# Mixer A of a hybrid network on one core: the low part of the queries made later, one query group ahead of the first scores, output groups started on x's parts

## The chip, the core and the metric

The kernel runs on one core of a Trainium2 chip. Five engines work side by side, each through its own queue in order: PE (TensorE), DVE (VectorE), ACT (ScalarE), POOL (GpSimd) and SP (SyncE, which issues the transfers). They wait for each other by semaphores. The metric is device time in microseconds, the median of several runs.

## What is computed

The reference is a network of two blocks. The part that the change touches is mixer A, the first layer's grouped attention with axial rotation, on 512 tokens of x and 256 of a context (model width 1024, 16 heads of 64):

```python
px = hx @ w_in
q, k, v, z = ...                                   # columns of px
q = apply_axial_rope(rms_norm(q, q_g), cos, sin)
k = apply_axial_rope(rms_norm(k, k_g), cos, sin)
k_all = concatenate([kc, k]); v_all = concatenate([vc, v])
s = einsum(q, k_all) * ATTN_SCALE
o = softmax(s) @ v_all                             # blocks of 128 queries
yx = (o * silu(z)) @ w_out
...                                                # the context: own queries, over kc and vc alone
x = x + g_x * yx ; ctx = ctx + g_c * yc
```

All is in 32-bit floats. Products that need full precision are split into a high and a low part (fp32r): a projection is three matmuls, high x high, low x high and high x low.

## The kernel before

A plan is made first: a list of items such as ("score", "a", n), written in order by ordinary Python, and each engine's program then takes from it the items in which it has a share. So one order sets five queues. The change touches mixer A's attention.

*Steps.* There are 8 pairs of heads (0 to 7) and for each pair 6 tiles of 128 queries, four of x (against 768 keys, "large") and two of the context (256 keys, "small"). Step n is tile n % 6 of pair n // 6, so 48 steps, 0 to 47. `attention` runs the softmax as a pipeline: in step n PE makes score n (L1530, 12 matmuls, 6 in a small tile), the outputs of step n - 2 ("pv", L1565) and the transposes of the probabilities of n - 1 ("turn", L1540), for two heads h. DVE takes the maximum (L2154) and its negative (L2163), ACT the exponential with its sum (L1814), DVE the reciprocal (L2170), POOL scales (L2544); turned probabilities are copied from PSUM by ACT (L1824) and DVE (L2179); DVE keeps the output, times the gate (L2190). Scores of both heads fill PSUM banks 0 to 3, a single buffer, so a score waits for the exponentials of the step before. Turns use banks 4 and 5, and outputs also bank 5. A step needs its own PE work and leaves PE idle unless something fills the gaps.

*Fill.* The generator `fill_a` yields projection blocks ("proj": 3 matmuls, one of 8 k; L1442 to L1444; 512 columns for x, j = 0, and 256 for the context, j = 1). `fill_in` draws from it in the two halves of a step (before and after the turn of head 1), up to a share of the remaining work by the step's weight (1.0, small tiles 0.7); `PAUSE` ends a half's filling at once, and `BLOCK` says that nothing may be drawn. For pair p = 1 to 7 `fill_a` makes the query group (pair, 0), (pair, 1), then the gate group (pair, 0), (pair, 1). In the gate group hang the query's further steps: sums (L1507, L2114, POOL's power L2532), rotation (L1513, L2118, POOL's L2537, and the sum on DVE L2124), the high part (ACT, L1796), the low part (DVE, L2128), and the gate: tanh (ACT, L1804), product (DVE, L2134). After the low part the pair counts as ready and its first score may be made. "mod" units (L1455 and L1463) ride along. Pair 0's groups are made before the steps.

*Output groups.* At the end `begin_out` begins the output projection ("aout", m = 0 and 1, x's columns): for each k, the gated outputs of pair k are split into parts ("parts": ACT casts the high part, L1776; POOL for even k, L2518, and DVE for odd k, L2074, subtract the low one) into the buffers that held the projections' input. Hence parts wait until the gate groups are done with it.

*Weights.* A unit of weights is loaded by SP, then split in quarters: ACT casts (L1726), POOL subtracts (L2477). `tick` puts a quarter into the plan; the load of the unit after next follows the fourth quarter.

## Time and profile before

| | |
|---|---|
| median of 3 runs | 1638.76 us (1638.26 to 1641.87) |
| profiled execution | 1637.41 us, span from first to last instruction 1635.7 us |
| PE busy | 1551.2 us, 95% |
| DVE, ACT, POOL busy | 740.2, 623.5, 658.7 us |
| attention of mixer A | 107.9 to 459.2 us of the span |

The profile is of one execution. Rows of the timeline give an instruction's start, its duration, its form, how many of that form follow each other, and in brackets how long the engine was idle before it and on what it waited. Rows of windows give the busy time of each engine in a stretch and PEclk, the granted TensorE clock as a share of full speed.

### The profile page before, as it was taken

The numbers are of one execution on the slowest core, as the hardware profiler recorded it, in microseconds if no ns is written. First come the engines' busy times: TensorE is split into PE (matmuls) and PEld (weight loads), VectorE is DVE, ScalarE is ACT, GpSimd is POOL, SyncE is SP. The second block draws the span as 40 slices with busy tenths as digits, with TensorE's granted clock in tenths as the row PEclk, the third lists the DMA queues.
The fourth block names the chain that finished last, engine by engine and source line by source line (L and its number), as shares of the span: only waits on it lengthen the run. The fifth ranks groups of instructions, "written<-read, shape, count | busy, mean of one in ns | idle before, by whom it ended". The sixth has DMA issues, their size and how long they took to land.

```text
span 1635.7 us, 25366 instructions
## 1 busy us (share of the span) xinstructions
PE 1551.2 (95%) x10018; PEld 1227.2 (75%) x10018; DVE 740.2 (45%) x1717; ACT 623.5 (38%) x1303; POOL 658.7 (40%) x640
## 2 busy tenths in 40 slices
PE   5999999999898999999998899999999999999997
...
GB/s 396 47 60 52 31 49 53 53 52 27 72 123 103 78 78 78 104 78 110 72 104 52 78 92 73 100 52 103 52 78 78 90 66 78 52 52 27 78 98 57
DMA packets 22438, 129.80 MB, mean 79 GB/s; under 512 B 2480, under 2 KB 2608, under 8 KB 8368
## 3 DMA queue, kind: packets, MB, share of 16 engines
q1 hardware_dynamic: 22176, 127.92, 21.9%
...
## 4 chain that ended last, share of the span: by engine, by line
PE 81%; DVE 8%; ACT 3%; POOL 3%; issue 3%; DMA 1%; SPq 0%; POOLq 0%; DVEq 0%; ACTq 0%
PE PS L1442 15%; PE PS L1444 14%; PE PS L1443 14%; PE PS L1565 6%; PE PS L1540 6%; PE PS L1523 4%; PE PS L1696 3%; PE PS L1437 3%; PE PS L1438 3%; PE PS L1439 3%; PE PS L1530 3%; DVE sm L2154 2%; PE PS L1706 2%; PE PS L1618 1%; PE PS L1610 1%
## 5 line engine op out<-in xcount | busy, mean ns | idle before, releaser
L2477 POOL TENSOR_TENSOR WL<-W,WH 128x512 fp32r<-128x512 f32 x280 | 367.4, 1328 | 321.7 <-ACT WH L1726 321.4
L1442 PE MATMUL PS<-HX,WH 128*128 128x512 f32 x1008 | 420.5, 417 | 11.3 <-DVE LX L2067 3.7
L1444 PE MATMUL PS<-HX,WL 128*128 128x512 f32 x1008 | 398.6, 395 | 0.0
L1443 PE MATMUL PS<-LX,WH 128*128 128x512 f32 x1008 | 398.3, 395 | 0.0
L1442 PEld LDWEIGHTS PS<-HX,WH 128*128 128x128 f32 x1008 | 192.5, 191 | 62.7 <-issue 17.9
L1444 PEld LDWEIGHTS PS<-HX,WL 128*128 128x128 f32 x1008 | 192.1, 191 | 42.7
L1443 PEld LDWEIGHTS PS<-LX,WH 128*128 128x128 f32 x1008 | 192.7, 191 | 36.7 <-issue 3.4
L1726 ACT CAST WH<-W 128x512 fp32r<-128x512 f32 x296 | 172.0, 618 | 51.6 <-PE PS L1439 23.7
L1814 ACT ACTIVATE AR<-PS,sm 128x768 f32<-128x768 f32 (+4 forms) x160 | 115.7, 723 | 173.8 <-DVE sm L2159 101.1
L2154 DVE TENSOR_REDUCE sm<-PS 128x1 f32<-128x512 f32 (+4 forms) x224 | 149.9, 669 | 44.8 <-PE PS L1530 40.3
L2544 POOL TENSOR_SCALAR AR<-AR,sm 128x768 f32<-128x768 f32 (+1 forms) x96 | 77.1, 804 | 186.8 <-DVE sm L2170 186.8
L1540 PE MATMUL PS<-C,AR 128*128 128x128 f32 x608 | 101.4, 284 | 10.0 <-DVE AR L2190 9.9
L2544 POOL TENSOR_SCALAR XC<-XC,sm 128x512 f32<-128x512 f32 x64 | 45.0, 703 | 163.0 <-DVE sm L2170 163.0
L1824 ACT COPY AR<-PS 128x512 f32<-128x512 f32 (+1 forms) x112 | 62.2, 555 | 108.9 <-PE PS L1540 107.9
L1565 PE MATMUL PS<-AR 128*64 128x128 f32 x1408 | 96.8, 283 | 5.3 <-DVE AR L2179 3.6
L1540 PEld LDWEIGHTS PS<-C,AR 128*128 128x128 f32 x608 | 68.9, 141 | 43.4 <-issue 22.6
L1814 ACT ACTIVATE XC<-PS,sm 128x512 f32<-128x512 f32 x64 | 44.2, 690 | 145.0 <-DVE sm L2159 145.0
L1437 PE MATMUL PS<-WH,HX 128*128 128x256 f32 x320 | 94.9, 297 | 0.8 <-POOL WL L2477 0.8
L1565 PEld LDWEIGHTS PS<-AR 128*64 128x64 f32 x1408 | 77.2, 139 | 23.4 <-issue 11.8
L1439 PE MATMUL PS<-WL,HX 128*128 128x256 f32 x320 | 91.2, 285 | 0.0
L1438 PE MATMUL PS<-WH,LX 128*128 128x256 f32 x320 | 91.2, 285 | 0.0
L2547 POOL TENSOR_SCALAR AR<-AR,sm 128x128 f32<-128x128 f32 (+3 forms) x64 | 39.2, 612 | 111.8 <-DVE sm L2170 109.3
...
## 6 DMA issues: line engine op xcount, KB each, us to landing
...
```

Of the source, the lines that this page charges most:

```text
L1437: e.matmul(o, xh, wh, start=(k == 0), stop=False)
L1438: e.matmul(o, xl, wh, start=False, stop=False)
L1439: t = e.matmul(o, xh, wl, start=False, stop=(k == 7))
L1442: e.matmul(o, wh, xh, start=(k == 0), stop=False)
L1443: e.matmul(o, wh, xl, start=False, stop=False)
L1444: t = e.matmul(o, wl, xh, start=False, stop=(k == 7))
L1540: t = e.transpose(o[:, j * 128:j * 128 + 128], s.pb[h][:, (q0 + j) * 128:(q0 + j) * 128 + 128], c("id"))
L1565: t = e.matmul(s.out[h], s.values[h][j], s.pt[h][:, j * 128:j * 128 + 128], start=(j == 0 and s.first), stop=(j == nv - 1 and s.final))
L1726: e.copy(WH[:, PART[n], a:z], W[:, n % 2, a:z]).then_inc(*s_wh.by(n, q))
L1814: e.activation(s.pb[h][:, 0:s.n], PS[:, s.score[h]:s.score[h] + s.n], ACT.Exp, bias=smn[:, i % 4:i % 4 + 1], scale=(1.0 if s.scale is None ...
L2154: e.tensor_reduce(mx, x, AX.X, ALU.max).then_inc(*s_max.by(name, n, h))
L2477: e.tensor_tensor(WL[:, d, a:z], W[:, n % 2, a:z], WH[:, d, a:z].bitcast(F32), ALU.subtract).then_inc(*s_wl_pool.by(n, q))
```

## The change

Three things in mixer A. In `fill_a` the low part of a pair's queries is written behind block k = 5 of the gate group of the context instead of k = 1, and most pauses are gone. The query group (1, 0) is drawn ahead of the first score: an `AHEAD` mark is yielded behind it, and the caller draws up to the mark. The output groups are begun by a new `begin_out_a`: the part of x of pair 0 and 1 is made while the last gate group of the context still runs (parts of x now wait for the gate group of x alone), the parts of x are always two k ahead of their blocks, a context part follows its block, and there are no pauses. The work handed to `attention` is 890.9 instead of 946.8 units of 100 columns, over steps whose weights sum to 43.2: 20.6 instead of 21.9 for a step of weight 1. (One unit is three matmuls of 100 columns.)

```diff
-        def parts_a(k):
-            for j, (lo, hi) in enumerate(FULL):
-                after = [(s_gated, ("a", j)) if k == 7 else (s_post, ("a", 6 * k + 5)), (s_proj, ("az", 7, 1))]
-                parts("o", k, j, zT.at(k, lo, hi), after, "pool" if k % 2 == 0 else "dve")
+        def parts_a(k, j):
+            lo, hi = FULL[j]
+            after = [(s_gated, ("a", j)) if k == 7 else (s_post, ("a", 6 * k + 5)), (s_proj, ("az", 7, j))]
+            parts("o", k, j, zT.at(k, lo, hi), after, "pool" if k % 2 == 0 else "dve")
+
+        def begin_out_a():
+
+            un = Unit("aout", 0)
+            led = {(m, 0): bank(FA.take(("aout", m, 0), (s_res, ("aout", m, 0)))) for m in (0, 1)}
+            for k in range(2, 9):
+                if k < 7:
+                    yield from until(lambda: k in done_a)
+                    parts_a(k, 0)
+                for m in (0, 1):
+                    yield from pj(("aout", m, 0), un, 0, T, 128 * m, "o", led[m, 0], (k - 2,))
+                parts_a(k - 2, 1)
+            begun["aout"] = un, led
...
             for pair in range(1, 8):
                 yield from query_group(pair, 0, FX, {2: ride_mm, 6: ride_tr})
-                yield PAUSE
+                if pair == 1:
+                    yield AHEAD
                 yield from query_group(pair, 1, FC)
...
-                yield from gate_group(pair, 1, FC, {1: lambda: query_low(pair), **({3: ride_mm_x, 6: ride_tr} if pair == 7 else {})})
-                yield PAUSE
-            yield from begin_out("aout", "o", parts_a, done_a, FA)
+                last_ = {2: lambda: parts_a(0, 0), 3: ride_mm_x, 4: lambda: parts_a(1, 0), 6: ride_tr} if pair == 7 else {}
+                yield from gate_group(pair, 1, FC, {**last_, 5: lambda: query_low(pair)})
+            yield from begin_out_a()
...
-        attention("a", [s for pair in range(8) for s in steps_a(pair)], SA, TA, PbA, PTbA, OA, fill_a(), (8 * 14 * (T + LC) + 14 * T) / 100 + 5 * 3, posted_a, scored_a.add)
+        fill_ = fill_a()
+        while next(fill_) != AHEAD:
+            pass
+        attention("a", [s for pair in range(8) for s in steps_a(pair)], SA, TA, PbA, PTbA, OA, fill_, (8 * 14 * (T + LC) + 6 * T) / 100, posted_a, scored_a.add)
...
-        parts_a(7)
+        parts_a(7, 0)
+        parts_a(7, 1)
```

The changed kernel has 18 more lines, so its lines from here on are numbered 18 higher. ACT, around the first exponential (its table load; L1814 before, L1832 in the change), before:

```order
L1796 CAST XX_parts<-AR 128x768
L1726 CAST WH<-W 128x512 x2
L1804 ACTIVATE AR<-PS 128x256
L1814 ACT_TABLE_LOAD
L1814 ACTIVATE AR,sm<-PS,sm 128x768 x2
L1733 COPY AR<-PS 128x256
L1824 COPY AR<-PS 128x512
```

and in the change, from the high part of pair 0 (L1796, now L1814):

```order
L1814 CAST XX_parts<-AR 128x768
L1744 CAST WH<-W 128x512 x2
L1822 ACTIVATE AR<-PS 128x256
L1751 COPY AR<-PS 128x256
L1744 CAST WH<-W 128x512 x2
L1809 ACTIVATE AR<-PS 128x512
L1832 ACT_TABLE_LOAD
L1832 ACTIVATE AR,sm<-PS,sm 128x768 x2
L1744 CAST WH<-W 128x512 x2
L1809 ACTIVATE AR<-PS 128x256
```

A mod unit's row, two casts of weights (L1744) and the square of the raw queries (L1809) now stand ahead of it, and two more casts behind it.

DVE, from the gate of x (L2134) of pair 6 to the first maximum behind its low part (L2128, writing XX_parts), before:

```order
L2134 SCALAR_TENSOR_TENSOR AR<-AR,PS 128x512
L2154 TENSOR_REDUCE sm<-PS 128x1
L2163 TENSOR_SCALAR sm<-sm 128x1
L2190 SCALAR_TENSOR_TENSOR AR<-PS,AR 128x128
L2179 COPY AR<-PS 128x256
L2154 TENSOR_REDUCE sm<-PS 128x1
L2163 TENSOR_SCALAR sm<-sm 128x1
L2170 RECIPROCAL sm<-sm 128x1
L2128 TENSOR_TENSOR XX_parts<-AR,XX_parts 128x768
L2170 RECIPROCAL sm<-sm 128x1
L2154 TENSOR_REDUCE sm<-PS 128x1
```

and in the change (gate L2152, low part L2146), from the output kept in the last step of pair 5 on:

```order
L2208 SCALAR_TENSOR_TENSOR AR<-PS,AR 128x128
L2197 COPY AR<-PS 128x256
L2172 TENSOR_REDUCE sm<-PS 128x1
L2181 TENSOR_SCALAR sm<-sm 128x1
L2188 RECIPROCAL sm<-sm 128x1
L2142 TENSOR_TENSOR AR<-AR 128x512
L2188 RECIPROCAL sm<-sm 128x1
L2152 SCALAR_TENSOR_TENSOR AR<-AR,PS 128x512
L2146 TENSOR_TENSOR XX_parts<-AR,XX_parts 128x768
L2172 TENSOR_REDUCE sm<-PS 128x1
L2181 TENSOR_SCALAR sm<-sm 128x1
```

Before, a step's maxima and two reciprocals (L2170) stood between gate and low part on one side and the score's first maximum on the other; now the low part stands behind both reciprocals (L2188) and the gate, directly ahead of the maximum (L2172) of the score that needs it.

PE, from score 43 on, before (score L1530, outputs L1565, turns L1540, block L1442 to L1444):

```order
L1530 MATMUL PS<-AR_parts,XX_parts 128x512 x6
L1530 MATMUL PS<-AR_parts,XX_parts 128x256 x6
L1565 MATMUL PS<-AR 64x128 x4
L1540 MATMUL PS<-C,AR 128x128 x12
L1530 MATMUL PS<-AR_parts,XX_parts 128x512 x6
L1530 MATMUL PS<-AR_parts,XX_parts 128x256 x6
L1565 MATMUL PS<-AR 64x128 x12
L1540 MATMUL PS<-C,AR 128x128 x6
L1442 MATMUL PS<-HX,WH 128x512
L1443 MATMUL PS<-LX,WH 128x512
L1444 MATMUL PS<-HX,WL 128x512
L1442 MATMUL PS<-HX,WH 128x512
```

and in the change (L1548, L1583, L1558, L1460 to L1462):

```order
L1548 MATMUL PS<-AR_parts,XX_parts 128x512 x6
L1548 MATMUL PS<-AR_parts,XX_parts 128x256 x6
L1583 MATMUL PS<-AR 64x128 x4
L1558 MATMUL PS<-C,AR 128x128 x6
L1460 MATMUL PS<-HX,WH 128x512
L1461 MATMUL PS<-LX,WH 128x512
L1462 MATMUL PS<-HX,WL 128x512
L1460 MATMUL PS<-HX,WH 128x512
L1461 MATMUL PS<-LX,WH 128x512
L1462 MATMUL PS<-HX,WL 128x512
L1558 MATMUL PS<-C,AR 128x128 x6
L1460 MATMUL PS<-HX,WH 128x512
```

Before, score 44 followed the turns of step 43 directly, and the first blocks of the output stood in step 44; now two blocks stand in each half of step 43, and they run out earlier.

## Rows read from the trace of the kernel before

**Rows 1.** The page: busy time, share and instructions of PE and the others.

```profile
PE 1551.2 (95%) x10018; PEld 1227.2 (75%) x10018; DVE 740.2 (45%) x1717; ACT 623.5 (38%) x1303; POOL 658.7 (40%) x640
```

**Rows 2.** Windows: length, busy of PE, PEld, DVE, ACT, POOL; PEclk; DMA share; GB/s.

```profile
107.90:459.20 351.30, 329.28 (x2799) 264.59 (x2797) 183.51 (x487) 170.13 (x364) 151.04 (x150) 0.98 0.15 53
```

**Rows 3.** Waits of PE, 105 to 465 us: in total, times, the longest.

```profile
PE PS L1540 <- DVE AR L2190: 9.9, 12, 2.8
PE PS L1565 <- DVE AR L2179: 3.6, 6, 1.2
```

**Rows 4.** Timeline of PE: rows behind a pause.

```profile
110.03 1.32 PE L1530 MATMUL PS<-AR_parts,XX_parts 64*128 64x512 f32 x12 [1.94 <-DVE AR L2134]
...
145.87 0.44 PE L1540 MATMUL PS<-C,AR 128*128 128x128 f32 x2 [2.81 <-DVE AR L2190]
...
191.35 0.44 PE L1540 MATMUL PS<-C,AR 128*128 128x128 f32 x2 [1.57 <-DVE AR L2190]
...
325.02 1.53 PE L1565 MATMUL PS<-AR 128*64 128x128 f32 x24 [1.08 <-DVE AR L2179]
...
413.61 2.29 PE L1530 MATMUL PS<-AR_parts,XX_parts 64*128 64x512 f32 x12 [2.12 <-DVE XX_parts L2128]
...
427.42 2.29 PE L1530 MATMUL PS<-AR_parts,XX_parts 64*128 64x512 f32 x12 [1.88 <-ACT AR L1814]
...
430.95 2.83 PE L1565 MATMUL PS<-AR 128*64 128x128 f32 x24 [1.25 <-DVE AR L2179]
```

**Rows 5.** Windows: three slow stretches, and a stretch between.

```profile
145.80:151.00 5.20, 5.13 (x32) 4.89 (x32) 2.41 (x8) 1.75 (x5) 1.58 (x2) 0.67 0.42 165
...
413.50:417.00 3.50, 3.39 (x21) 2.67 (x22) 1.06 (x2) 0.00 (x0) 0.00 (x0) 0.51 0.65 272
427.30:435.00 7.70, 6.33 (x44) 5.47 (x45) 3.94 (x8) 3.39 (x8) 5.24 (x5) 0.56 0.00 0
...
190.00:236.00 46.00, 42.50 (x365) 34.28 (x366) 24.46 (x66) 21.65 (x47) 18.37 (x18) 1.00 0.14 47
```

**Rows 6.** Timelines of PE and ACT: scores, second exponentials (ACT) and a block.

```profile
404.11 0.62 PE L1530 MATMUL PS<-AR_parts,XX_parts 64*128 64x256 f32 x6
...
407.64 0.57 ACT L1814 ACTIVATE AR<-PS,sm 128x256 f32<-128x256 f32 x1 [1.51 <-DVE sm L2163]
...
426.19 0.99 ACT L1814 ACTIVATE AR<-PS,sm 128x768 f32<-128x768 f32 x1 [0.75 <-DVE sm L2163]
...
436.51 0.48 PE L1442 MATMUL PS<-HX,WH 128*128 128x512 f32 x1
...
438.08 1.33 PE L1530 MATMUL PS<-AR_parts,XX_parts 64*128 64x512 f32 x12
...
443.34 1.00 ACT L1814 ACTIVATE AR<-PS,sm 128x768 f32<-128x768 f32 x1 [0.25 <-DVE sm L2163]
...
445.10 0.62 PE L1530 MATMUL PS<-AR_parts,XX_parts 64*128 64x256 f32 x6
```

**Rows 7.** Timelines of ACT and DVE: low parts, high part, gate and copy.

```profile
236.95 1.20 DVE L2128 TENSOR_TENSOR XX_parts<-AR,XX_parts 128x768 fp32r<-128x768 f32 x1 [0.18 <-issue]
...
322.59 0.82 ACT L1796 CAST XX_parts<-AR 128x768 fp32r<-128x768 f32 x1
...
323.94 0.69 DVE L2134 SCALAR_TENSOR_TENSOR AR<-AR,PS 128x512 f32<-128x512 f32 x1 [1.87 <-ACT AR L1804]
...
324.55 0.42 DVE L2179 COPY AR<-PS 128x256 f32<-128x256 f32 x1
...
412.51 0.95 DVE L2128 TENSOR_TENSOR XX_parts<-AR,XX_parts 128x768 fp32r<-128x768 f32 x1
```

**Rows 8.** DMA, 95 to 140 us in 40 slices: busy tenths of the 16 engines.

```profile
DMA  0000000000000007697891000000000000000000
```

**Rows 9.** Timeline of PE: the last score and the last outputs.

```profile
452.11 0.62 PE L1530 MATMUL PS<-AR_parts,XX_parts 64*128 64x256 f32 x6
...
458.59 0.66 PE L1565 MATMUL PS<-AR 128*64 128x128 f32 x8 [0.46 <-ACT AR L1824]
```

2 lines of the change are left out of this document (1 added, 1 removed).

## The prediction

> **What bounds the kernel now.** I read the page first, then the busy times by stage, the waits of TensorE and its timeline. [rows 1] PE is busy for 95% of the span. In mixer A's attention, 107.9 to 459.2 us [rows 2], which is all that the change touches, it is busy for 329.3 of 351.3 us, a busy time that overstates its use since pipelined matmuls overlap. So time can only be won from PE's pauses there and from stretches at the lower clock. The waits of PE in this stage come to 21.6 us in seven groups: the first two hold 13.5 [rows 3], the other five, on exponentials, copies, the low part and the gate, 8.1; the timeline shows where the long ones are [rows 4]. Three stretches ran at a lower granted clock [rows 5]: 0.67 over 5.2 us, 0.51 over 3.5 us and 0.56 over 7.7 us, worth 1.7, 1.7 and (its wait of 1.25 us taken out) about 2.8 us of lost work, each behind a pause of 1.9 to 2.8 us. Together 27.8 us are lost in the stage. About 2.5 of that are pauses of 0.2 to 0.3 us that any order has (turns that wait for the kept output after a small tile), so 25.3 us are at stake.
>
> **The limit of a step.** A step has its own PE work, and fill (blocks of projections) between. From score to score the step at 438.08 took 7.02 us with four blocks of 512 columns; two blocks take 1.57 us, from the block at 436.51 to the score at 438.08 [rows 6], 0.69 each and 0.2 for starting, so the own work is some 4.27 us with the starts in it. The next score waits for the second exponential: this ends 6.26 us after the score's start (438.08 to 444.34) [rows 6], and a score follows such an end by 0.24 us (426.19 + 0.99 = 427.18, then the score at 427.42) [rows 4, 6]. So a large tile cannot be under 6.5 us, and needs 2.2 us of fill. The last small tile of a pair (404.11 to 408.21) cannot be under 4.3 us, and has 2.5 us of own work. Fill above these limits costs only itself, and the total of fill is the same in both kernels. What counts is fill that is missing in one step, and waits for the query chain.
>
> **Part 1, a group ahead and the start.** The first score waited 1.94 us for the gate product on VectorE [rows 4]. Now eight blocks and a mod unit stand ahead of it (5.5 and 1.4 us): the wait goes, 1.9 gained. The cost is on ScalarE: two casts of weights and the square stand ahead of the first exponential, and the cast waits for the load that is issued once GpSimd's splits are through, near 111.4. The transfers of this and the next unit run from 111.9 to 119 before [rows 8]; the first has landed at about 116.3, the first exponential comes at about 118.0 instead of 117.4 (107.9 + 6.9 + score 1.3 + maximum 1.2), and PE, with only 2.9 us of fill then, waits about 1.1 us. The third step has two blocks (1.4 us) where 2.2 are needed: 0.8 lost. The chain rotation, high part, gate of pair 1 stands ahead of the fourth step now, where the score is long (1.33 us) and hides nearly all: 0.25. Pair 1 lost 2.81 and 1.7 of clock before. Sum: from 6.45 to 2.15.
>
> **Part 2, pairs 2 to 7.** Pauses are fewer and a step's share of fill is 20.6 instead of 21.9 (by the kernel's own count), so the query chain shifts against the steps. Two mechanisms, both in the trace. First, the gate ahead of something urgent on VectorE: high part 0.82, tanh 0.6, gate 0.69, and then the copy of the turned probabilities, for which PE's outputs waited 1.08 us [rows 4, 7]. Pair 2 gets this form, with the high part only behind the second exponential: 6.26 + 0.75 + 0.6 + 0.7 + 0.4 = 8.7 us, where PE stands ready at 7.1, so 1.6 (its gate wait of 1.57 goes). Pair 3 keeps the old form ahead of a small tile, 0.5 instead of 1.57, since the rotation is done earlier. Second, the low part. In pairs 4 to 7 it now stands on VectorE behind the reciprocal of the step's second exponential, one block ahead of the score that needs it. So this score comes no sooner than 0.15 + 0.94 + 0.15 = 1.24 us behind the end of that exponential, where 0.24 is the old limit, and later where the gate is in front. Worked through the queues: pair 4: the gate delays the maxima, score 24 comes at 11.7 us behind score 22, for 10.0 us of work: 1.7. Pair 5: exponential 4.15, high part to 4.95, tanh 5.5, gate 6.2, low 7.2, score at 7.4; work 5.7: 1.6. Pair 6: high part to 5.5, gate 6.7, low 7.6, score 7.75; work 6.4: 1.35. Pair 7: the low half of a part of x (odd, so on VectorE) waits there for its ScalarE cast at 7.9 and stands ahead of the low part: low 9.5, score 9.6; work 7.9: 1.7. Fill missing at large tiles (1.4 us in steps 33 and 39, 1.8 in step 9, 1.4 in step 13, which is the one behind two small tiles) adds 0.3 and 0.4 (pair 2), 0.7 (pair 3), 0.1 each (pairs 4, 5), 0.8 and 0.8. Sum by pair, before to now: 1.6 to 2.3, 1.65 to 1.2, 1.7 to 1.8, 1.5 to 1.7, 1.2 to 2.15, 2.4 to 2.5: 10.05 to 11.65. These pairs gain nothing; they lose 1.6.
>
> **Part 3, the tail (steps 42 to 47).** Before, steps 42 and 43 have parts but no output blocks, and PE waits 1.88 us for the exponential and 1.25 for a copy that stands behind the parts on VectorE [rows 4], at 1.2 GHz; with the clock (1.7 and 2.8), 0.66 and the last 0.92 it is 9.2. Now the 14 blocks stand in every half. Step 42: the part of k = 3 stands ahead of the next maximum on VectorE and ends near 8.1 us behind score 42, where the maximum could start at 6.9: 1.4 us at the turn. Steps 44 to 46: 0.4, 0.8 (two blocks only), 0.2. Step 47 has no fill left: from its score to the last output it took 7.07 us with 1.37 of blocks and 0.92 of waits [rows 9], so 4.78 of work, while its chain of exponential, reciprocal, scale, turn, copy takes about 6.7: 1.9. Sum 4.7, so 9.2 to 4.7. Moved blocks cost the same where they land.
>
> **The sum.** By places it was 6.45 + 10.05 + 9.2 = 25.7, by the totals 25.3, and I take the smaller; now it is 2.15 + 11.65 + 4.7 = 18.5. For the clock I add 1.5: one drop, as at 145.8 [rows 5], since pairs 7 and step 42 have two pauses of 1.4 to 1.7 us within 10 us. So 20.0 against 25.3: 5.3 us less. The profiled execution took 1637.41 us (span 1635.7), the median is 1.35 above it. Span 1630.4, time 1638.76 - 5.3 = **1633.5 us**. Unknown costs: a low-part wait is between 0 (where the exponential ends early) and 2.1 (the one at 413.61), four of them 0 to 8.4, taken at 6.35; the clock between 0 and 6.2.
>
> **Two rules of the Trainium skill.** [rows 4, 5] Pauses of 0.2 to 1.6 us between 190 and 236 us left the clock at 1.00, that is 2.4 GHz; 1.88 and more had rows at 1.2 GHz behind them, though 1.94 at 110.03 had not. The Trainium skill, "TensorE: Matmul & The Clock Gate", section "A second HAM failure mode: psum-queue depth-cycling", says that frequent micro-idles between groups of matmuls are enough to make the clock oscillate. By that rule the new order, with about as many short waits, would throttle again, which is the slower rival below; by the rows it would not. [rows 7] The low part took 1.20 us at 236.95 and 0.95 at 412.51, with the same operands. The Trainium skill, "GPSIMD Engine Reference", section "Specifications", says that GpSimd shares SBUF interfaces with VectorE and that instructions with two SBUF inputs contend. By it four low parts on the path could cost 0.25 more each, 1.0 in all, and the time would be 1634.5.
>
> **The rivals.** *A, the new waits eat the gain*: the low-part waits are 2.1 us each as at 413.61 instead of 1.6 (+2.0) and the clock drops behind two more of them (+3.4, at 1.7 each): 1633.5 + 5.4 = 1638.9, no difference. For it: the chain is the one that made 2.12 us before, and now stands so in four pairs. Against: four more blocks stand between high part and score. *B, slower by the clock*: the waits ahead of scores 24, 30, 36, 42, the start and step 43 each reach some 1.9 us, from where rows at 1.2 GHz follow; six drops of 1.7 to 2.8, some 2.2 each, less the 1.5 that is in the sum, and 0.4 longer each: 13.2 - 1.5 + 2.4 = 14.1, less if only four fall: four give +8.9, 1642.4. Against it: gaps of 1.57 to 1.62 us left the clock alone. *C, everything is covered*: where the low part's wait is hidden and the clock never falls, 6.35 - 0.8 and 1.5 more are gained: 1626.5. For it: before, pair 6 shows no wait at all in this chain. Against: the reciprocal in front is a fixed place in the queue. *D, the change does not do what it says*: the order shows all three moves, so it gets no chance of its own.
>
> **How the numbers follow.** Forecast 0.57 (1629.5 to 1635.4), A 0.25 (1635.5 to 1642), B 0.09, C 0.09. Within 0.2%, 3.3 us, is about what a measurement of this kernel can tell from no change. Faster 0.66, the same 0.25, slower 0.09. The range leaves out B and the far half of C: 1627.5 to 1639.
>
> **What would show it.** Right: the first score without a wait on VectorE's gate; waits of the score on the low part (VectorE, XX_parts) at four pairs, 1.2 to 1.8 us each; one outputs-on-copy wait near 1.6 us in pair 2; granted clock above 0.98 in the stage; stage end to end 346 us instead of 351.3. Wrong: score waits on the low part under 0.5 us, rows near 0.5 behind pauses shorter than 1.8 us, or a first exponential later than 119 us, which would be the load at the start.

## The result and the profile after

The change took 1646.42 us (median of 13 runs, 1639.49 to 1650.01) where the kernel before took 1639.05 us in the same series (13 runs, 1637.55 to 1641.87). The ratio is 1.0042, its 95% interval 1.0034 to 1.0051: 7 us slower, where 5.3 us less was forecast, and outside the range of 1627.5 to 1639.0. The profiled execution of the change took 1642.32 us, 4.1 under the median of its runs; its span is 1640.6 us, 4.9 more than before. Of these 4.9 the stage holds 5.7, the part of the program ahead of it 1.5 (the stage begins at 109.40 instead of 107.90; the mean clock up to there is 0.89 instead of 0.92), and the part behind it, 1174.2 us instead of 1176.5, gives 2.3 back. The change touches neither of the two.

The windows of the change (length; busy PE, PEld, DVE, ACT, POOL; PEclk; DMA share; GB/s) show the whole stage, which answers to [rows 2], and three stretches that ran below full clock, as in [rows 5]:

```profile
109.40:466.40 357.00, 327.67 (x2798) 262.40 (x2797) 182.40 (x487) 169.77 (x364) 152.74 (x150) 0.99 0.15 53
...
123.00:130.00 7.00, 6.35 (x35) 5.50 (x35) 3.22 (x8) 4.59 (x11) 4.92 (x5) 0.76 0.18 47
425.00:430.00 5.00, 3.40 (x23) 2.44 (x24) 3.36 (x10) 3.24 (x8) 1.13 (x2) 0.89 0.52 213
430.00:440.00 10.00, 9.68 (x58) 7.09 (x59) 4.56 (x11) 5.06 (x12) 4.71 (x5) 0.89 0.00 0
```

The stage took 357.0 us where it took 351.3 [rows 2], 5.7 more; PE was busy for 1.6 us less in it, and its clock was a little higher. So the time did not go to the clock but into pauses. The stretches lost 1.7 us (0.24 of 7.0), 0.6 and 1.1, 3.4 in all, against 6.2 before.

The waits of PE in the change from 105 to 472 us (which line waited for which, us in total, times, the longest), the view of [rows 3]:

```profile
PE PS L1548 <- ACT AR L1832: 5.7, 7, 2.6
PE PS L1473 <- DVE AR L2152: 4.9, 4, 1.5
PE PS L1548 <- DVE XX_parts L2146: 4.4, 4, 1.4
PE PS L1583 <- DVE AR L2197: 3.8, 6, 1.4
PE PS L1558 <- DVE AR L2208: 3.5, 9, 0.8
PE PS L1583 <- ACT AR L1842: 2.5, 3, 1.9
PE PS L1460 <- DVE sm L2024: 1.9, 2, 1.3
...
```

With three groups of 1.7, 0.3 and 0.2 us that are left out they come to 28.9 us; before it was 21.6. The largest group of before, turns on the kept output (9.9 us at L2190 [rows 3], here L2208), went down to 3.5. In its place stand the matmuls of a mod unit (L1473) that wait for the gate product (L2152), scores (L1548) that wait for the low part (L2146) and blocks (L1460) that wait for the mod unit's addition (L2024): 4.9, 4.4 and 1.9 us. Waits and clock together went from 27.8 to 32.3 us, which is 4.5 of the 5.7; the other 1.2 no wait shows.

The timeline of PE in the change gives their places. First the start, which answers to the first two rows of [rows 4], then the row that stands for the 1.57 at 191.35 there, then some of the later ones, to the end:

```profile
116.65 1.33 PE L1548 MATMUL PS<-AR_parts,XX_parts 64*128 64x512 f32 x12
123.65 1.09 PE L1548 MATMUL PS<-AR_parts,XX_parts 64*128 64x512 f32 x8 [2.60 <-ACT AR L1832]
...
192.36 1.53 PE L1583 MATMUL PS<-AR 128*64 128x128 f32 x24 [1.37 <-DVE AR L2197]
...
330.41 1.31 PE L1548 MATMUL PS<-AR_parts,XX_parts 64*128 64x512 f32 x12 [1.33 <-DVE XX_parts L2146]
...
419.87 1.07 PE L1473 MATMUL PS<-W,sm 128*32 128x256 f32 x16 [1.49 <-DVE AR L2152]
...
423.63 1.32 PE L1548 MATMUL PS<-AR_parts,XX_parts 64*128 64x512 f32 x12 [1.43 <-DVE XX_parts L2146]
...
428.00 0.50 PE L1460 MATMUL PS<-HX,WH 128*128 128x512 f32 x1 [1.28 <-DVE sm L2024]
...
448.35 1.53 PE L1583 MATMUL PS<-AR 128*64 128x128 f32 x24 [1.08 <-DVE AR L2197]
...
463.81 0.66 PE L1583 MATMUL PS<-AR 128*64 128x128 f32 x8 [1.89 <-ACT AR L1842]
```

Pair 7 has the most of them. Within 9.6 us, PE waits for the gate product before it can make the mod unit, for the low part before it can make score 42, and for the mod unit's addition before the first output block: 4.2 us. DVE's timeline of the change shows the other side:

```profile
419.12 0.69 DVE L2152 SCALAR_TENSOR_TENSOR AR<-AR,PS 128x512 f32<-128x512 f32 x1 [1.85 <-ACT AR L1822]
421.93 0.69 DVE L2092 TENSOR_TENSOR LX<-AR,HX 128x512 fp32r<-128x512 f32 x1 [2.12 <-ACT HX L1794]
422.54 0.95 DVE L2146 TENSOR_TENSOR XX_parts<-AR,XX_parts 128x768 fp32r<-128x768 f32 x1
424.96 0.96 DVE L2172 TENSOR_REDUCE sm<-PS 128x1 f32<-128x768 f32 x1 [1.47 <-PE PS L1548]
```

DVE is idle for 1.85 and 2.12 us in between. No engine is short of time here. A chain stands alone, because all fill that should lie over it has been drawn. One of its links is not the query's: the 2.12 us ahead of L2092 are a wait for ScalarE's cast of a part of x, which the new `begin_out_a` puts between the gate product and the low part. In e3 below, without these parts, the low part follows the gate product at once, and score 42 does not wait, though the mod unit waits 1.49 us there too:

```profile
414.19 0.69 DVE L2158 SCALAR_TENSOR_TENSOR AR<-AR,PS 128x512 f32<-128x512 f32 x1 [1.85 <-ACT AR L1828]
414.79 0.95 DVE L2152 TENSOR_TENSOR XX_parts<-AR,XX_parts 128x768 fp32r<-128x768 f32 x1
...
417.20 1.33 PE L1554 MATMUL PS<-AR_parts,XX_parts 64*128 64x512 f32 x12
```

So the 1.43 us at score 42 come from the new start of the output groups together with the late pair; either one put back takes them away (e3, e5), and e6, at e3's pace with the new start, has them.

### The profile page after: what moved, and what is told of

Its sections match the earlier page's. It is cut to its first block, busy times and chain, and to the rows that moved or that the text cites. A ratio compares the mean times of both kernels' runs of the same rounds, so it can differ in the third digit from the quotient of the medians.

```text
span 1640.6 us, 25367 instructions
## 1 busy us (share of the span) xinstructions
PE 1549.2 (94%) x10018; PEld 1226.3 (75%) x10018; DVE 736.9 (45%) x1717; ACT 622.9 (38%) x1303; POOL 660.8 (40%) x640
## 4 chain that ended last, share of the span: by engine, by line
PE 79%; DVE 8%; ACT 5%; issue 3%; POOL 3%; DMA 1%; SPq 0%; POOLq 0%; DVEq 0%; ACTq 0%
PE PS L1460 14%; PE PS L1461 14%; PE PS L1462 14%; PE PS L1583 6%; PE PS L1558 6%; PE PS L1541 4%; PE PS L1714 3%; PE PS L1455 3%; PE PS L1456 3%; PE PS L1457 3%; DVE sm L2172 2%; PE PS L1548 2%; PE PS L1724 2%; PE PS L1473 1%; PE PS L1636 1%
## 5 line engine op out<-in xcount | busy, mean ns | idle before, releaser
L1460 PE MATMUL PS<-HX,WH 128*128 128x512 f32 x1008 | 421.6, 418 | 12.2 <-DVE LX L2092 2.6
L1462 PE MATMUL PS<-HX,WL 128*128 128x512 f32 x1008 | 399.0, 396 | 0.0
L1460 PEld LDWEIGHTS PS<-HX,WH 128*128 128x128 f32 x1008 | 193.2, 192 | 62.9 <-issue 16.3
L1462 PEld LDWEIGHTS PS<-HX,WL 128*128 128x128 f32 x1008 | 192.8, 191 | 42.9
L1744 ACT CAST WH<-W 128x512 fp32r<-128x512 f32 x296 | 171.8, 618 | 56.0 <-DMA W<-in_wu 25.5
L1832 ACT ACTIVATE AR<-PS,sm 128x768 f32<-128x768 f32 (+4 forms) x160 | 115.7, 723 | 171.4 <-DVE sm L2177 101.1
L2172 DVE TENSOR_REDUCE sm<-PS 128x1 f32<-128x512 f32 (+4 forms) x224 | 149.9, 669 | 52.6 <-PE PS L1548 48.1
L1558 PE MATMUL PS<-C,AR 128*128 128x128 f32 x608 | 100.6, 284 | 5.5 <-DVE AR L2208 3.5
L1583 PE MATMUL PS<-AR 128*64 128x128 f32 x1408 | 95.0, 279 | 7.1 <-DVE AR L2197 3.8
L1832 ACT ACTIVATE XC<-PS,sm 128x512 f32<-128x512 f32 x64 | 44.2, 690 | 145.0 <-DVE sm L2177 145.0
L1558 PEld LDWEIGHTS PS<-C,AR 128*128 128x128 f32 x608 | 69.0, 141 | 39.0 <-issue 22.1
L1583 PEld LDWEIGHTS PS<-AR 128*64 128x64 f32 x1408 | 75.8, 137 | 25.1 <-issue 11.9
L2565 POOL TENSOR_SCALAR AR<-AR,sm 128x128 f32<-128x128 f32 (+3 forms) x64 | 39.1, 612 | 111.8 <-DVE sm L2188 109.0
## 6 DMA issues: line engine op xcount, KB each, us to landing
AR<-in_wu SPq DMA_DIRECT2D x8, 1024.0 KB, 11.5
XC<-in_xt SPq DMA_DIRECT2D x1, 1024.0 KB, 14.2
```

The costliest lines, as they stand in the source:

```text
L1460: e.matmul(o, wh, xh, start=(k == 0), stop=False)
L1462: t = e.matmul(o, wl, xh, start=False, stop=(k == 7))
L1558: t = e.transpose(o[:, j * 128:j * 128 + 128], s.pb[h][:, (q0 + j) * 128:(q0 + j) * 128 + 128], c("id"))
L1583: t = e.matmul(s.out[h], s.values[h][j], s.pt[h][:, j * 128:j * 128 + 128], start=(j == 0 and s.first), stop=(j == nv - 1 and s.final))
L1744: e.copy(WH[:, PART[n], a:z], W[:, n % 2, a:z]).then_inc(*s_wh.by(n, q))
L1832: e.activation(s.pb[h][:, 0:s.n], PS[:, s.score[h]:s.score[h] + s.n], ACT.Exp, bias=smn[:, i % 4:i % 4 + 1], scale=(1.0 if s.scale is None ...
```

## The experiments

Two views are used for all of them. The *lead*, from the emitted order alone, is the fill drawn when the first score of pair p comes, less what must have been drawn by the low part of pair p, in units (a block of 512 columns is 5.12, of 256 columns 2.56). `attention` draws on without a limit until the pair is ready, so the lead is never under 2.56: such a pair's low part stands directly ahead of its score. The *lost time*, from the PE timeline, is the stage less a fixed price for PE's own work, the same 313.1 us for every kernel. Only its differences mean something, and small ones do not: each is read from a single profiled execution, and the clock moves it. PE made the same work in the same order up to step 40 in e5 and e10, and pair 0 took 45.8 us in the one and 44.2 in the other. "Stage" is taken here from the last block ahead of the first scores that all orders share, so it is 351.0 us before and 356.8 in the change. "Pair p" in lost times is the six steps of that pair.

| kernel | units a step | lead at pairs 1 to 7 | stage | lost | median |
|---|---|---|---|---|---|
| before | 21.9 | 26 26 26 26 15 10 2.6 | 351.0 | 37.9 | 1639.05 |
| change | 20.6 | 49 36 20 2.6 2.6 2.6 2.6 | 356.8 | 43.7 | 1646.42 |
| e1_low_early | 20.6 | 59 46 31 10 2.6 2.6 2.6 | 358.1 | 45.0 | 1647.85 |
| e2_no_group_ahead | 21.6 | 20 36 20 2.6 2.6 2.6 2.6 | 356.1 | 43.0 | 1647.62 |
| e3_old_output_start | 21.0 | 61 49 36 20 10 2.6 2.6 | 353.0 | 39.9 | 1640.27 |
| e4_mod_later | 20.6 | as the change | 363.9 | 50.8 | 1652.71 |
| e5_pace_219 | 21.9 | 61 67 77 64 56 49 31 | 349.0 | 35.9 | 1639.62 |
| e6_pace_210 | 21.0 | 61 49 36 20 10 2.6 2.6 | 352.3 | 39.1 | 1642.15 |
| e7_before_pace_206 | 20.6 | 10, then 2.6 six times | 366.2 | 53.1 | 1665.39 |
| e8_before_no_pauses | 21.9 | 31 46 46 31 20 10 2.6 | 354.3 | 41.2 | 1642.70 |
| e9_before_low_later | 21.9 | 15 15 15 15 5 2.6 2.6 | 353.2 | 40.1 | 1642.84 |
| e10_front_loaded | 21.9, then even | 61 67 77 64 56 49 20 | 346.9 | 33.8 | 1639.18 |
| e11_front_raw_behind | as e10 | as e10 | 346.0 | 32.9 | 1638.00 |
| e12_front_216 | 21.6, then even | 61 67 64 56 49 31 10 | 347.3 | 34.2 | 1636.90 |

The kernel before was run beside them: 1639.23 us (e1 to e4), 1637.92 (e5 to e8), 1639.18 (e9 to e11) and 1639.32 (e12). The ratios below are to that one; between series they compare better than the medians.

**e1: is it the place of the low part?** The changed kernel with the low part at its old block.

```diff
-                yield from gate_group(pair, 1, FC, {**last_, 5: lambda: query_low(pair)})
+                yield from gate_group(pair, 1, FC, {**last_, 1: lambda: query_low(pair)})
```

> The change with the low part of the queries back behind block k = 1 of the gate group. Theory W (the loss is the sum of the named waits of PE, each of them made by what now stands next to what): the four waits of the score on the low part (4.4 us in the profile of the change) go, and of the outputs' wait behind gate and copy little changes: 3 to 4.5 us less than the change, so about 1.0020 of the kernel before. Rival C (the excess over the profile is the clock, which falls more often where pauses are many): the mean granted clock of the runs rises from 0.975 to above 0.977 and the gain is larger than the waits taken away, 6 us. Rival N: the low part was not on the path, the next wait on the same chain (gate, maximum) takes its place: less than 1.5 us.

Measured: 1647.85 us, ratio 1.0053 (1.0041 to 1.0065). The waits of its scores on the low part, in its waits of PE:

```profile
PE PS L1548 <- DVE XX_parts L2146: 7.3, 4, 2.8
```

and two of them in its PE timeline:

```profile
330.59 2.29 PE L1548 MATMUL PS<-AR_parts,XX_parts 64*128 64x512 f32 x12 [2.75 <-DVE XX_parts L2146]
...
378.25 1.31 PE L1548 MATMUL PS<-AR_parts,XX_parts 64*128 64x512 f32 x12 [2.11 <-DVE XX_parts L2146]
```

The waits got longer, 7.3 us against 4.4. An earlier low part lets the pair be ready four blocks earlier, so `attention` stops drawing four blocks earlier and less fill lies over the same chain. The low part is still directly ahead of the score in pairs 5 to 7. So putting it back does not help: the wait belongs to the pair being late. (The profiled execution of e1, 1652.56 us, is its slowest, and its stage holds a stretch at 0.54 of the clock, so the 1.3 us in the stage say nothing.)

**e2: is it the group drawn ahead?** The changed kernel without the mark, all groups drawn inside the steps, the count raised by that group.

```diff
-                if pair == 1:
-                    yield AHEAD
...
-        fill_ = fill_a()
-        while next(fill_) != AHEAD:
-            pass
-        ... fill_, (8 * 14 * (T + LC) + 6 * T) / 100, ...
+        ... fill_a(), (8 * 14 * (T + LC) + 14 * T) / 100, ...
```

> The change without the query group ahead of the first score. In the change the start and pair 0 lose 6.5 us beside their work, before 7.25. Theory W: the start loses the 2.6 us behind the first exponential and gets the 1.94 us behind the gate again; but all chains of the pairs shift by a group against the steps, so the waits of the mod matmuls behind the gate (4.9 us) and of the low part (4.4 us) come elsewhere: between 3 us less and 2 us more than the change. Rival: the group ahead was what helped, and the time goes up by the 4.3 us that the prediction gave to it.

Measured: 1647.62 us, ratio 1.0052 (1.0040 to 1.0065). In its waits of PE the gate wait at the first score is back, and the turn that waited 2.8 us while pair 1's queries were made; the groups on the gate for the mod unit and on the low part are those of the change:

```profile
PE PS L1553 <- DVE AR L2203: 5.5, 9, 2.8
PE PS L1468 <- DVE AR L2147: 4.9, 4, 1.5
PE PS L1543 <- DVE XX_parts L2141: 4.4, 4, 1.4
...
PE PS L1543 <- DVE AR L2147: 1.9, 1, 1.9
```

The stage is 0.7 us shorter than the change's, not longer, and the ratio's interval overlaps that of the change. The group drawn ahead moved its pauses (from the first score and that turn to score 1 and small ones); no gain of it shows.

**e3: is it the new start of the output groups?** The changed kernel with the old `begin_out` and its pause, and 15 units more in the count (this also makes the pace 21.0).

```diff
-                last_ = {2: lambda: parts_a(0, 0), 3: ride_mm_x, 4: lambda: parts_a(1, 0), 6: ride_tr} if pair == 7 else {}
+                last_ = {3: ride_mm_x, 6: ride_tr} if pair == 7 else {}
...
-            yield from begin_out_a()
+            yield PAUSE
+            yield from begin_out("aout", "o", parts_old, done_a, FA)
...
-        ... (8 * 14 * (T + LC) + 6 * T) / 100, ...
+        ... (8 * 14 * (T + LC) + 6 * T) / 100 + 5 * 3, ...
```

> The change with the output groups begun as before (both parts of a pair at once, behind the last gate group, with pauses, and no parts in the gate group). Theory W: the tail is within 1 us of the change, since both tails lose about 11 us beside their work, one by waits at the lower clock, one by short waits; the wait of the first output block on the mod unit's bank (1.28 us) goes and those of 1.9 to 2 us with clocks near 0.5 come back. Rival: the new start of the output groups is worth the 4.5 us that were predicted, and the time goes up by that.

Measured: 1640.27 us, ratio 1.0012 (1.0000 to 1.0024). This took most of the loss away, but two things had been altered. Its lost time from step 36 on is 18.4 us against 17.7 in the change; all of the gain and more lies ahead of it, in pairs that the output groups do not touch. Within the last steps one thing is exchanged for another: score 42 no longer waits (1.43 in the change), but score 43 waits 2.17 us for the exponential and a turn 3.16 us for the kept output. That pointed to the number, which e6 separates.

**e4: are the mod units in the way?** In the change a mod unit's matmuls wait for the gate's PSUM bank. Here they ride three blocks later.

```diff
-                yield from query_group(pair, 0, FX, {2: ride_mm, 6: ride_tr})
+                yield from query_group(pair, 0, FX, {5: ride_mm, 7: ride_tr})
```

> The change with the mod unit's matmuls riding behind block k = 5 of a query group instead of k = 2 (turns behind k = 7 instead of 6). They take PSUM bank 7, which the gate product of the pair before frees; in the profile of the change they wait 1.14, 1.15 and 1.15 us for it in pairs 5 to 7. Theory W: these 3.4 us go (the fourth, 1.49, in the last gate group, stays): 2.5 to 3.5 us less than the change. Rival N: what takes their place (the step behind has less fill) gives back most: under 1 us. Rival C: more than 5 us, with a higher mean clock.

Measured: 1652.71 us, ratio 1.0087 (1.0074 to 1.0099). Its waits of PE:

```profile
PE PS L1460 <- DVE sm L2024: 6.8, 7, 1.4
...
PE PS L1481 <- ACT AR L1751: 3.4, 2, 2.9
...
PE PS L1473 <- DVE AR L2152: 1.5, 1, 1.5
```

The wait on the gate fell from 4.9 to 1.5 us, as it should. The waits on the low part stay (4.5 us). Seven blocks now wait for the mod unit's addition instead (6.8 us), because the unit holds the bank that the next group wants, and its turns (L1481) wait 3.4 us for ScalarE's copy. The wait was a symptom, and its old place was the better one.

**e5 and e6: is it the pace?** The changed kernel with the count alone altered, to the share per step of before (21.9), and by e3's 15 units (21.0).

```diff
-        ... (8 * 14 * (T + LC) + 6 * T) / 100, ...
+        ... (8 * 14 * (T + LC) + 14 * T) / 100 + 5 * 3, ...      # e5
+        ... (8 * 14 * (T + LC) + 6 * T) / 100 + 5 * 3, ...       # e6
```

> The changed kernel with one number put back: the work that is spread over the 48 steps is counted as before the change (43.2 units of time more), so that each step takes 21.9 units of other work, as before, and not 20.6. Order of the streams as in the change; by the emitted order the low parts of pairs 1 to 7 then end in steps 3, 8, 14, 20, 27, 33 and 40, that is 2 to 4 steps ahead of their first scores, and the last output blocks end in step 44, which leaves steps 45 to 47 without other work. Theory P (the pace makes the chain of each pair just late): TensorE's waits on the low part and on the gate for the mod unit (4.4 and 4.9 us in the change) fall under 2 us together, the last steps lose 2 to 3 us more for want of work, and the time is 1638 to 1642, ratio to before 0.999 to 1.002. Theory N (the new order costs by itself, whatever the pace): the same waits stand within 1 us of 9.3 together, and the time is 1645 to 1649, ratio 1.004 to 1.006. Theory C (the granted clock behind pauses): the waits fall as under P, and yet the time is above 1644, with the stage's clock under 0.98.

> The changed kernel with 15 units more in that count, 21.0 units a step instead of 20.6: the number that the run with the old start of the output groups also had. It tells that run's gain (1640.3 against 1646.4) apart: new start of the output groups or pace. Theory P: about the time of that run, 1639 to 1643, waits on the low part under 1.5 us, on the gate for the mod unit about 2.6 us. Theory O (it was the new start of the output groups): the pace gives nothing, waits and time as in the change, 1645 to 1648, and the steps from 36 on lose as much as in the change (17.7 us).

Measured: e5 1639.62 us, ratio 1.0011 (1.0000 to 1.0023); e6 1642.15 us, ratio 1.0019 (1.0008 to 1.0031). The window of e5's stage:

```profile
109.40:458.40 349.00, 326.21 (x2794) 262.17 (x2794) 182.63 (x487) 170.14 (x363) 152.49 (x150) 0.99 0.16 54
```

and its largest waits of PE:

```profile
PE PS L1548 <- ACT AR L1832: 9.5, 9, 2.7
PE PS L1558 <- DVE AR L2208: 6.0, 11, 1.5
```

One number took 7.8 us off the stage and 6.8 off the median (5 by the ratios, 1.0042 and 1.0011), and it fell where the theory of the pace put it: the groups on the low part and on the gate are gone from the list. The low part ends 19.6, 14.2, 13.3 and 6.8 us ahead of the first scores of pairs 4 to 7, where it ended 0.14 or 0.15 us ahead in the change. e6 lies between, with the pauses of the change in pairs 6 and 7 alone (2.6 us on the gate, 1.9 on the low part). It has e3's number and the new start of the output groups: its stage is 0.7 us shorter than e3's, its ratio 0.0007 higher with overlapping intervals, so e3's gain was the number. What the new start is worth by itself is not settled; between these two it is under 2 us. From step 42 to the end 10.8 us are lost in the change, 10.9 in e6 and 11.3 in e5, so the steps left without other work in e5 cost 0.5, not 2 to 3. The pace therefore explains most or all of what the change lost, and none of the gain that was forecast: e5 is no faster than the kernel before.

**e7: the pace in the other kernel.** The kernel before, with the change's share.

```diff
-        ... (8 * 14 * (T + LC) + 14 * T) / 100 + 5 * 3, ...
+        ... (8 * 14 * (T + LC) + 6 * T) / 100, ...
```

> The kernel before with the change's count alone: 20.6 units a step, all else untouched. By the emitted order the low parts of pairs 4 to 7 then come in the second half of the step just ahead of their scores (steps 23, 29, 35, 41), each of which carries 8.7 us of other work where 2 to 4 is usual. Theory P: waits of 1 to 3 us at the first scores of pairs 4 to 7 and at their gates, the stage 6 to 15 us longer, 1645 to 1655, ratio 1.004 to 1.010. Theory N: the pace alone is worth little, under 3 us: 1639 to 1642.

Measured: 1665.39 us, ratio 1.0166 (1.0147 to 1.0185), further than either theory. Its largest group in the waits of PE:

```profile
PE PS L1530 <- DVE XX_parts L2128: 16.4, 7, 4.5
```

and the worst place in its PE timeline:

```profile
433.04 2.29 PE L1530 MATMUL PS<-AR_parts,XX_parts 64*128 64x512 f32 x12 [4.46 <-DVE XX_parts L2128]
```

Scores wait for the low part in seven places: 4.46 us in the last pair, 2.0 in the mean of the other six. The stage grew by 15.2 us. The rest of the program grew by 10 more in this profile (1186.5 us behind the stage, 1176.5 before), which the pace should not touch. The granted clock covers it: span times mean clock is 1661.7 x 0.971 = 1613.5 against 1635.7 x 0.977 = 1598.1, which is 15.4 more, the growth of the stage; why the clock was lower is open. The change has the same number and loses 5.8 us in the stage, not 15.2. The number is harsher here: this kernel has 946.8 units to draw by its own count, 56 more than the 890.9, and its planned pauses hold fill back, so that by the emitted order some 49 units stand in each of steps 23, 29, 35 and 41, and 51 in step 47. So e7 confirms the direction, not the size.

**e8: the pauses.** The kernel before without its planned pauses inside a pair; the one ahead of the output groups stays.

```diff
                 yield from query_group(pair, 0, FX, {2: ride_mm, 6: ride_tr})
-                yield PAUSE
...
                 yield from gate_group(pair, 1, FC, ...)
-                yield PAUSE
+            yield PAUSE
             yield from begin_out("aout", ...)
```

> The kernel before, pace and order as before, with the four planned pauses in each pair's other work taken out (those behind the query group's first tile, the gate's first group and its second). Then each half step takes up what the next unit needs at once. Theory S (pauses only space the work; without them it is spread more evenly): the emitted order leaves 6 us instead of 16 in steps with too little work, and the time falls 2 to 5 us: 1634 to 1637. Theory L (without them the chain is as late as in the change, because the low part lands in step 41 directly ahead of its score and the last output blocks crowd steps 42 to 47): waits on low part and gate as in the change, 5 to 9 us, and the time is 1641 to 1646.

Measured: 1642.70 us, ratio 1.0024 (1.0012 to 1.0035). Both theories put the gain or loss in the spread of fill. The emitted order leaves 10 us less missing fill, yet 3.3 us more are lost. Two places carry them. Pair 0 lost 7.2 us against 5.2, but that is the clock: from 111 to 118 us it was at 0.76, 1.7 us of loss, behind the same pause of 1.93 us that left it at 1.00 in the kernel before. The rest is pair 7 with its chain in a row, from its PE timeline:

```profile
417.12 1.32 PE L1529 MATMUL PS<-AR_parts,XX_parts 64*128 64x512 f32 x12 [2.80 <-DVE XX_parts L2127]
...
433.85 2.83 PE L1564 MATMUL PS<-AR 128*64 128x128 f32 x24 [2.22 <-DVE AR L2178]
```

These two waited 2.12 and 1.25 us before. So counting missing fill, which the prediction had done, does not price an order. Nor does the lead alone: it is higher here than before in five pairs and lower in none, and the time is longer.

**e9: the low part later, in the kernel before.**

```diff
-                yield from gate_group(pair, 1, FC, {1: lambda: query_low(pair), ...})
+                yield from gate_group(pair, 1, FC, {5: lambda: query_low(pair), ...})
```

> The kernel before with the low part of each pair's queries put behind block 5 of the gate's second group instead of block 1, all else as before. By the emitted order it stands in step 5 of each pair, the last one ahead of the scores that need it, two or more blocks behind where it stood. Theory P (what counts is how far ahead of its score the low part ends): at the first score the slack of the kernel before, which waited on no low part in pairs 2 to 6, goes down by about 1.1 to 2.2 us, waits of 0 to 1 us at the scores of pairs 2 to 6 and 1 to 2 us in pair 7, sum 1 to 5 us, 1639 to 1643. Theory L (the position itself costs what the change lost): waits of 1.4 us in each of pairs 4 to 7, sum 6 us or more, 1644 to 1648.

Measured: 1642.84 us, ratio 1.0026 (1.0016 to 1.0037). At the scores of pairs 1 to 4 the low part now ends 0.26 to 0.29 us ahead instead of 5 to 7, and the four pairs that lead up to these scores lose what they lost before (5.20, 3.64, 3.59 and 3.58 us against 5.16, 3.63, 3.59 and 3.64). So a low part that is just in time costs nothing. The 2 us more lie in pair 4 (3.9 against 2.9) and in the last steps (13.1 against 11.1), where one turn waits 3.17 us for the kept output; pair 6 gives 0.9 back. Waits on the low part are 1.1 us in two pairs, not 6: the second theory falls.

**e10, e11, e12: a pace that is quick first and even later.** Fill left for the tail has a use only once pair 7 is ready. So the count is raised until then and lowered to what is left afterwards. e11 also issues the raw product of the group ahead (DVE, L2126 in the change) behind the first two maxima; e12 is e11 at 21.6 units.

```diff
-                    until_ = spent[0] + (work - spent[0]) * todo[n][2] / left
+                    w_ = work - 56 if name == "a" and 7 in ready_q else work
+                    until_ = spent[0] + (w_ - spent[0]) * todo[n][2] / left
...
-        ... (8 * 14 * (T + LC) + 6 * T) / 100, ...
+        ... (8 * 14 * (T + LC) + 6 * T) / 100 + 56, ...          # e10, e11; both 44 in e12
...
+            if held:
+                yield AHEAD
             do("a_query_raw", pair, j)                           # e11, e12, for the group ahead
```

> The changed kernel at 21.9 units a step as in the run before that had this number, until the low part of pair 7 is made (step 40); from there on what is left (the output blocks) is spread evenly over the steps to the end, so that steps 45 and 46 have 1.4 us of blocks each where they had none. Theory P with a tail that wants filling: stage 1 to 3 us shorter than the 349.0 of that run, steps 42 to the end lose 9 to 10.5 us (11.3 there), 1636 to 1639 at the same granted clock. Theory F (the tail is bound by its exponentials, turns and the last two output products and takes no more work than it had): steps 42 to the end lose 11 us again, 1638 to 1641.

> As the front-loaded run, and the raw product of the group that is made ahead (pair 1, context side; 0.75 us on VectorE, which stood between the first scores and their first maximum) is issued behind the first two maxima. Its block in PSUM is free only then, and the next group takes the other one. Theory R (this product is what made the first maximum late): the first maximum 0.7 us earlier against the first score, the wait of TensorE at score 1 falls from 2.6 to 1.8 to 2.0 us, the stage is 0.5 to 0.9 us shorter than the front-loaded one. Rival T (the exponential's table load on ScalarE ends after the maximum either way): the wait at score 1 stays within 0.3 us of 2.6, stage unchanged.

> As the run with the raw product issued behind the first maxima, at 21.6 units a step instead of 21.9 until pair 7's low part is made: the count is 44 units over what is left, not 56. By the emitted order the low parts of pairs 1 to 7 end in steps 3, 8, 14, 21, 27, 34 and 41, that is those of pairs 4, 6 and 7 one step later than there, and steps 42 to 44 have 1.4 us more of output blocks. Theory P (the low part has to end a step ahead; between there and the next step lies the edge): TensorE waits on no low part up to pair 6 and 0 to 1 us at step 42, the tail loses 1 to 1.5 us less, the stage is 344.5 to 346.5 and the time 1635.5 to 1638.5. Rival E (the edge is already crossed in step 41): 1.4 us or more on the low part and 1 us or more on the gate at step 42, stage 347 to 349, 1638 to 1640.

Measured: e10 1639.18 us, ratio 0.9998 (0.9990 to 1.0007); e11 1638.00 us, ratio 0.9991 (0.9982 to 1.0000); e12 1636.90 us, ratio 0.9982 (0.9971 to 0.9993). Blocks left for the last steps brought the tail's loss from 11.3 to 9.3 us in e10 against e5, and pair 6 took 1.4 of it back. What the stage gained over e5, 2.1 us, cannot be put down to them: pair 0, where the two orders are the same, is 1.6 us shorter in e10, since its clock stayed up behind the pause at score 1 (2.62 us, and 2.67 in e5, whose window has 0.76 as in the change):

```profile
123.00:130.00 7.00, 6.68 (x48) 6.00 (x49) 3.96 (x11) 4.72 (x11) 5.64 (x7) 1.00 0.23 74
```

and e5's clock was 0.97 from 420 to 458 us where e10's was 1.00. The intervals of the two ratios overlap. The start is plain in the timelines. The rows are ACT and DVE of the kernel before, where ScalarE has its table load done and waits 1.93 us for the maximum, then of the change, then of e11:

```profile
109.39 1.28 ACT L1814 ACT_TABLE_LOAD   x1
112.61 0.99 ACT L1814 ACTIVATE AR<-PS,sm 128x768 f32<-128x768 f32 x1 [1.93 <-DVE sm L2163]
```

```profile
119.39 1.28 ACT L1832 ACT_TABLE_LOAD   x1
119.41 0.75 DVE L2126 TENSOR_SCALAR AR<-PS,V 128x512 f32<-128x512 f32 x1 [3.29 <-ACT AR L1809]
120.07 0.95 DVE L2172 TENSOR_REDUCE sm<-PS 128x1 f32<-128x768 f32 x1
121.31 0.99 ACT L1832 ACTIVATE AR<-PS,sm 128x768 f32<-128x768 f32 x1 [0.63 <-DVE sm L2181]
```

```profile
118.67 0.96 DVE L2173 TENSOR_REDUCE sm<-PS 128x1 f32<-128x768 f32 x1 [1.88 <-PE PS L1549]
119.53 1.28 ACT L1833 ACT_TABLE_LOAD   x1
120.82 0.99 ACT L1833 ACTIVATE AR<-PS,sm 128x768 f32<-128x768 f32 x1
```

```profile
123.00:130.00 7.00, 6.97 (x49) 6.19 (x50) 4.62 (x12) 4.91 (x10) 5.28 (x6) 1.00 0.22 60
```

(The last row is e11's window behind score 1.) The first maximum came 3.42 us behind the start of score 0 (116.65) in the change and 1.34 us behind it (117.33) in e11, since the product no longer stands ahead; nor does ScalarE's square of the same group. PE's wait at score 1 fell from 2.60 (2.62 in e10) to 1.30 us, more than expected, because the square had moved too and the table load began 0.5 us sooner behind the score. The load is now what the exponential waits for: it ends at 120.81, the maximum was ready at 119.88. In the change it was the other way round. e12 has its low part in step 41, just ahead of score 42, and pays neither on it nor on the gate: its list of waits has no row for either. It beats the change clearly and the kernel before by 0.18%, with an interval that excludes no difference; e10 and e11 cannot be told from the kernel before. Its stage is 1.3 us longer than e11's all the same and its time 1.1 shorter; what tells these two apart is the granted clock of the executions (0.9766 in the mean of its 12, 0.9746 in e11's 11), so no order between them is claimed.

## Why the prediction was wrong, by its steps

By places, in us, from the pauses and the clock in the timeline of the change; the small pauses, up to 0.43 us, stand apart. A pair here is the stretch in which its queries are made, as in the prediction:

| | before | forecast | measured |
|---|---|---|---|
| start, pairs 0 and 1 | 6.45 | 2.15 | 6.7 |
| pairs 2 to 7, up to score 42 | 10.05 | 11.65 | 13.3 |
| tail | 9.2 | 4.7 | 7.1 |
| clock elsewhere | | 1.5 | in the rows above |
| small pauses | 2.5 | 2.5 | 5.1 |

The column of before is the prediction's. Sorted by the rule of the last column, the rows before hold 3.5 us of small pauses and 8.8 in pairs 2 to 7, so those pairs lost 4.5 us more, not 3.3. The forecast is off by 9.8 us in waits and clock: 4.5 at the start, 2.6 in the small pauses, 1.7 in pairs 2 to 7, and 0.9 in the tail once the 1.5 of clock, which the prediction expected about step 42, is counted there.

**What held.** The first score waits for no gate. There are four waits of scores on the low part, in pairs 4 to 7, at 0.77, 1.33, 0.87 and 1.43 us (forecast 1.2 to 1.8, in the sum 6.35 against 4.4), and the wait of the outputs on the copy in pair 2 is 1.37 (forecast 1.6). The order had been read rightly.

**The step that failed in its mechanism: Part 2's "a step's share of fill is 20.6 instead of 21.9 (by the kernel's own count), so the query chain shifts against the steps".** A shift was costed, at 1.6 us for these pairs, and each pair by itself. It is not a shift but a debt that grows. A pair draws 122.9 units of fill, and its six steps (weights 5.4) draw 5.4 x 20.62 = 111.4 in the change and 118.4 before. The lead therefore falls by about 11.5 units a pair instead of 4.5; whole blocks and the group ahead add to it at the front, and before the change the planned pauses hold it near 26 for four pairs (e8, without them, has 46). Counted in the order it reads 49, 36, 20 and then 2.6 four times. From pair 4 on, each chain from rotation to low part stands alone once a pair, with everything that belongs to it. The low part was only the part of it that the prediction priced. What it left out were its neighbours in the same chain: mod units whose PSUM bank waits for the gate product (1.14, 1.15, 1.15 and 1.49 us) and blocks behind the mod unit's addition (0.62 and 1.28). The prediction looked for them in no step. That its sum for these pairs, 11.65, comes near the 13.3 is partly luck: 5.5 us of mod unit and block waits were missing, while the low part was put 1.95 too high and missing fill at 3.2, where the one such wait of any size is 0.74 (at 216.44). e5 shows the cause, with only the number altered: the groups on the low part and the gate gone, 0.9 left on the addition, 7.8 us of stage back. e7 shows the direction from the other side.

**Part 1, the start: the gain was 0 instead of 4.3.** This is the largest single term of the miss. The wait at score 1 was put at 1.1 us and was 2.60. The first exponential came at 121.31 where 118.0 had been forecast, and later than the 119 that the prediction had named as a sign of being wrong; but it was not the load. The stage begins 1.5 us later here, and ScalarE's casts began at 117.74, 8.3 us behind that beginning, where the forecast of 116.3 had them 8.4 behind it. What failed is the step from the casts to the exponential: 1.7 us forecast, 3.57 measured. The prediction had the first maximum done by 117.4, beside the casts. On VectorE the raw product (0.75 us) stands ahead of it and waits for ScalarE's square, so that product and maximum follow one after the other behind the square; the exponential waited 0.63 us more for them, as the rows above show. The table load of 1.28 us had no term either, and ended at 120.67: it cost nothing here, since the maximum was later still. The pause of 2.60 had a stretch at 0.76 of the clock behind it, 1.7 us. Then 0.78, 0.30, 0.48 and 0.83 in pairs 0 and 1. e11 confirms the queue: without the product ahead the wait is 1.30. It does not show that the 1.7 us of clock belong to the pause, for in e10 the clock stayed at 1.00 behind 2.62 us.

**Part 3, the tail: a gain of 2.1 instead of 4.5.** The clock gained (1.7 lost against 4.5). From score 42 to the end it took 45.57 us before and 42.73 in the change, but four blocks of the context's gate group (1.4 us) and the mod unit's matmuls (1.07 us) now stand ahead of it, so the lost time there fell by 0.3 only, from 11.1 to 10.8. "Moved blocks cost the same where they land" is true and was the trap. The 14 output blocks do not fill steps 42 to 47: by the emitted order steps 45 and 46 have two each and step 47 none. The wait of the last outputs is 1.89 us, as forecast (1.9); those of 1.28 and 1.08 ahead of it were not, while the 1.4 expected at the turn of step 42 was 0.32. e10 loses 2.0 us less in its tail than e5 with the blocks spread to the end, by estimate 1.1 of it by the clock (38 us at 0.97 instead of 1.00).

**The small pauses** came to 5.1 us. They had been carried over at 2.5 as pauses "that any order has"; by the same sorting they were 3.5 before. e5 still has 6.0 us of turns on the kept output in 11 pauses. Part of that is now in a place where a step has more room, but I have no run that separates it.

**The rivals.** A came nearest in kind (new waits eat the gain) and B in size (1642.4 us with four drops, 1647.6 with six), but neither by its mechanism. B took its time from the clock, and the clock of the stage was higher than before. The psum rule that was weighed is answered by the same rows. In the change PE paused more (28.9 us) and the clock of the stage was 0.99 against 0.98. The Trainium skill, "TensorE: Matmul & The Clock Gate", section "A second HAM failure mode: psum-queue depth-cycling", tells of a kernel whose clock oscillated because of frequent micro-idles. More of them did not lower the clock of this stage. Nor did the low parts cost 0.25 us more each: all eight took 0.94 to 0.96 us, where one of before took 1.20 [rows 7]. The Trainium skill, "GPSIMD Engine Reference", section "Specifications", lists contention with GpSimd for VectorE's instructions with two SBUF inputs; these eight rows show none.

**A gain in the stage that the total does not show.** e11's stage is 5.0 us shorter than before's, its time 1.2. Over all executions e11 has a mean span of 1635.9 us at a mean clock of 0.9746, the kernel before beside it 1637.3 at 0.9763; multiplied, 1594.3 against 1598.5, which is 4.2 less. (Such a product is an estimate: pauses do not grow with the clock.) So about 3 us are lost to a lower clock elsewhere. e5 reads the same way: 1638.3 x 0.9740 against 1636.6 x 0.9763 is 2.1 less, where its stage is 2.0 shorter and its median 1.7 longer. For the change it is 1644.1 x 0.9755 = 1603.8 in the mean of its 13 executions against 1598.1 in the profiled one of before: 5.7 more, as much as the stage, and the rest of the 7.4 us of the median is clock. In the profiled executions it is visible in the windows at the same place of the program, some 60 to 80 us behind the stage, in the kernel before, in e12 and in e11:

```profile
519.00:539.00 20.00, 15.29 (x90) 12.47 (x89) 15.01 (x31) 9.49 (x17) 8.83 (x10) 0.83 0.16 53
```

```profile
516.00:536.00 20.00, 15.30 (x90) 12.47 (x89) 13.04 (x29) 7.66 (x14) 6.85 (x8) 0.83 0.15 53
```

```profile
516.00:536.00 20.00, 15.30 (x91) 12.88 (x90) 13.82 (x30) 8.08 (x15) 7.44 (x9) 0.74 0.15 53
```

PE's busy time in it is nearly the same, and the clock is 0.83, 0.83 and 0.74. Whether the shorter stage brings this about, or chance, these runs cannot say: e12, with nearly the same stage, has the clock of before.
